# A hybrid pooling, state-space and mixture-of-experts layer: where the second half of the down matrices is fetched, and the last product and scaling by tiles

## The reference

```python
hx2 = modulate(rmsnorm(x, g_ffn), x_sh2, x_sc2)
eidx, gate = route(hx2, w_router, b_router)          # best group, two experts inside it
hid = silu(xb @ w_gate[e]) * (xb @ w_up[e])          # w_gate, w_up: 1024 x 512 per expert
y   = hid @ w_down[e]                                # w_down: 512 x 1024 per expert
x   = x + x_g2 * y                                   # y weighted by the two gates
return rmsnorm(x, g_final)                           # x * rsqrt(mean(x*x) + 1e-6) * g_final
```

## Time and profile before

| | us |
|---|---|
| median of 3 runs | 661.68 (659.23 to 661.77) |
| the profiled execution | 661.11 |
| its span, first to last instruction | 659.3 |
| TensorE busy | 588.4 (89%) |
| VectorE busy | 196.1 (30%) |
| ScalarE busy | 132.0 (20%) |
| GpSimd busy | 53.3 (8%) |

### The profile page before, as it was taken

The page is one execution under the profiler, slowest core; times in us unless marked ns, Lnnn a source line. Parts: engine busy times, 40 slices in busy tenths (PEclk is TensorE's granted clock), DMA queues, the critical chain, the costliest instruction groups (busy, mean ns, idle before and its releaser), DMA issues.

```text
span 659.3 us, 9355 instructions
## 1 busy us (share of the span) xinstructions
PE 588.4 (89%) x3770; PEld 249.9 (38%) x3770; DVE 196.1 (30%) x426; ACT 132.0 (20%) x226; POOL 53.3 (8%) x103
## 2 busy tenths in 40 slices
PE   1999968889899997899799879979997997899995
PEld 0454544455553342234233323423342342234331
DVE  7998458988730020002001000200100010002003
ACT  8661312031213111012020201111021102012111
POOL 3894000012010000000000000000000000000000
PEclk9999979999979999999799989989998999999999
DMA  8993999998779999999999999999999999999951
GB/s 330 418 402 110 319 327 292 401 410 351 299 281 409 422 419 421 422 417 422 422 421 420 423 421 421 420 421 422 422 422 422 423 421 421 421 421 375 403 227 64
DMA packets 43609, 249.02 MB, mean 378 GB/s; under 512 B 4776, under 2 KB 7480, under 8 KB 17216
## 3 DMA queue, kind: packets, MB, share of 16 engines
q1 hardware_dynamic: 41240, 243.93, 91.2%
q10 hardware_dynamic: 1992, 3.68, 1.7%
q0 software_dynamic: 352, 1.07, 0.5%
HBM read 244.46 MB, written 2.11 MB: 374 GB/s over the span
## 4 chain that ended last, share of the span: by engine, by line
PE 56%; DMA 21%; DVE 2%; issue 1%; SPq 0%; ACT 0%; POOL 0%; DVEq 0%
PE ps L863 21%; DMA wts<-in_w_up 21%; PE ps L903 17%; PE ps L835 5%; PE ps L841 5%; PE ps L799 2%; PE ps L711 1%; PE ps L879 1%; PE ps L759 1%; PE ps L727 1%; SPq L243 0%; PE ps L864 0%; DVE rc L1204 0%; DVE ra L1589 0%; PE ps L791 0%
## 5 line engine op out<-in xcount | busy, mean ns | idle before, releaser
L863 PE MATMUL ps<-wts,ra 128*64 128x512 f32 x512 | 242.5, 626 | 34.2 <-DMA wts<-in_w_up 33.0
L864 PE MATMUL ps<-wts,ra 128*64 128x512 f32 x512 | 242.6, 626 | 0.0
L863 PEld LDWEIGHTS ps<-wts,ra 128*64 128x64 f32 x512 | 70.0, 143 | 180.3 <-issue 133.5
L903 PE MATMUL ps<-wts,ra 128*32 128x512 f32 x512 | 111.4, 593 | 0.0
L903 PE MATMUL ps<-rc,ra 128*32 128x512 f32 x512 | 111.4, 593 | 0.0
L1204 DVE TENSOR_TENSOR ra<-ra,ps 128x256 f32<-128x256 f32 x32 | 13.5, 422 | 268.7 <-ACT ra L1150 268.6
L1144 ACT COPY ra<-ps 128x512 f32<-128x512 f32 x32 | 33.6, 1050 | 218.6 <-PE ps L864 218.6
L864 PEld LDWEIGHTS ps<-wts,ra 128*64 128x64 f32 x512 | 70.0, 143 | 0.0
L903 PEld LDWEIGHTS ps<-wts,ra 128*32 128x32 f32 x512 | 29.1, 110 | 73.2 <-issue 73.2
L1204 DVE TENSOR_TENSOR cb<-ps,ra 128x512 f32<-128x512 f32 x32 | 22.1, 692 | 103.4 <-PE ps L903 103.4
L1139 ACT COPY ra<-ps 128x512 f32<-128x512 f32 x32 | 18.8, 586 | 148.4 <-PE ps L835 148.4
(11 more groups left out here) (226 smaller groups left out, 509.4 us busy)
## 6 DMA issues: line engine op xcount, KB each, us to landing
wts<-in_w_up SPq DMA_DIRECT2D x64, 1024.0 KB, 15.5
wts<-in_w_gate SPq DMA_DIRECT2D x64, 1024.0 KB, 13.4
wts<-in_w_down SPq DMA_DIRECT2D x30, 1024.0 KB, 8.6
rc<-in_w_down SPq DMA_DIRECT2D x30, 1024.0 KB, 12.4
wts<-in_w_mod SPq DMA_DIRECT2D x16, 1024.0 KB, 13.4
r<-in_w_mod SPq DMA_DIRECT2D x6, 1024.0 KB, 10.9
wts<-in_w_out SPq DMA_DIRECT2D x2, 2048.0 KB, 11.5
wts<-in_w_in SPq DMA_DIRECT2D x2, 1024.0 KB, 19.8
```

The lines of the kernel that those rows point to most:

```text
L863: pe.matmul(ps[0:64, 4 + b, :], st, Wg[b][:, k, :], start=(k == 0), stop=(k == KD - 1))
L864: mm = pe.matmul(ps[64:128, 4 + b, :], st, Wu[b][:, k, :], start=(k == 0), stop=(k == KD - 1))
L903: mm = pe.matmul(ps[32 * j:32 * j + 32, BANKS[n], :], hid[:, j, f, SLOTS * t:SLOTS * t + SLOTS], Wd[j][:, f, 512 * h:512 * h + 512], start ...
```

## The change

1. SP's list. In the loop the second down halves of a round are issued behind experts three and four (j = 2, 3) of that round: `downs(i, 0)`, `second_two(i)`, `downs(i, 1)`, `next_two(i)`. In the last round both halves come behind them: `second_two(last_four)`, `downs(last_four, 0)`, then the pieces of f = 2 and f = 3.
2. In the last round the four tiles of each f are multiplied in the order 0, 2, 1, 3 (both halves of the first 128 tokens, then of the second), VectorE takes them in that order, and the last scatter is four matmuls, each of which waits for its own tile. The first square waits for two of them, the second for all four.
3. The final scaling is taken apart: VectorE multiplies by g_final and the constant 32 (the root of 1,024) as soon as the square of those tokens is read; the multiplication by the inverse root of the sum is done in a second step, three tiles on ScalarE and one on VectorE. GpSimd adds 1,024 times epsilon to the sum in place of dividing by 1,024. Three stores are SP's, one is ScalarE's.
4. Two semaphores of the start are one (`consts_set`), and `ss3_ready` is merged into `ss2_ready`.

```diff
@@ sync
             with sp.Fori(1, last_four) as i:
                 downs(i, 0)
+                second_two(i)
                 downs(i, 1)
-                second_two(i)
                 next_two(i)
+            second_two(last_four)
             downs(last_four, 0)
-            second_two(last_four)
             sp.wait_ge(S("down_mm"), 4 * last_four)
             for f in (2, 3):
                 down_load_one(sp, lambda j: (4 * last_four + j) % NE, f)
-            for t in range(NT):
-                sp.wait_ge(S("fin_ready"), 2 * t + 1)
-                store(sp, t, 0)
+            for h in range(2):
+                sp.wait_ge(S("fin_act"), h + 1)
+                store(sp, 0, h)
+            sp.wait_ge(S("fin_ready"), 1)
+            store(sp, 1, 1)
@@ gpsimd
-            gp.wait_ge(S("mhalf_set"), 1)
+            gp.wait_ge(S("consts_set"), 2)
...
+            gp.dma_start(gfb, g_final.rearrange("(a d) -> a d", a=1).broadcast_to([P, D])).then_inc(S("gf_in"), 16)
+            for t in range(NT):
+                gp.wait_ge(S("ss2_ready"), NT + t + 1)
+                gp.tensor_scalar(ms2[:, 2 + t:3 + t], ms2[:, 2 + t:3 + t], float(D * EPS), None, ALU.add).then_inc(S("ms2_ready"), 1)
+                gp.wait_ge(S("ms2_ready"), NT + t + 1)
+                gp.tensor_tensor(rstd2[:, 2 + t:3 + t], ms2[:, 2 + t:3 + t], mhalf, ALU.pow).then_inc(S("rstd2_ready"), 1)
@@ tensor
+            TILE_ORDER = (0, 2, 1, 3)
...
-                    for n in range(4):
+                    for n in (TILE_ORDER if last else range(4)):
...
-            pe.wait_ge(S("out_copy"), 4 * last_four + 6)
             pe.wait_ge(S("pt_copy"), last_four + 2)
-            scatter(0, True)
-            pe.wait_ge(S("out_copy"), 4 * last_four + 8)
-            for t in range(NT):
-                pe.matmul(ps[:, 2 * t + 1, :], PT[:, t, :], oS[:, 2 + t, :], start=False, stop=True,
+            for at, n in enumerate(TILE_ORDER):
+                h, t = n // 2, n % 2
+                pe.wait_ge(S("out_copy"), 4 * last_four + 5 + at)
+                pe.matmul(ps[:, 2 * t + h, :], PT[:, t, :], oS[:, n, :], start=False, stop=True,
                           skip_group_check=True).then_inc(S("y_ready"), 1)
@@ scalar
-            act.wait_ge(S("sil_zero"), 1)
+            act.wait_ge(S("consts_set"), 2)
...
-                act.wait_ge(S("y_ready"), t + 1)
+                act.wait_ge(S("y_ready"), 2 * t + 2)
...
-            for t in range(NT):
-                act.wait_ge(S("fin_ready"), 2 * t + 2)
-                store(act, t, 1)
+            for at, (t, h) in enumerate(((0, 0), (0, 1), (1, 0))):
+                act.wait_ge(S("rstd2_ready"), NT + t + 1)
+                act.wait_ge(S("gf_scaled"), at + 1)
+                v = xn2[:, t, 512 * h:512 * h + 512]
+                act.mul(v, v, rstd2[:, 2 + t:3 + t]).then_inc(S("fin_act"), 1)
+            act.wait_ge(S("fin_act"), 3)
+            store(act, 1, 0)
@@ vector
-            four_out(last_four)
+            four_out(last_four, (0, 2, 1, 3))
             dve.wait_ge(S("gf_in"), 16)
             for t in range(NT):
-                dve.wait_ge(S("rstd2_ready"), 3 + t)
+                dve.wait_ge(S("ss2_ready"), NT + t + 1)
                 for h in range(2):
                     c0 = slice(512 * h, 512 * h + 512)
-                    dve.scalar_tensor_tensor(xn2[:, t, c0], ps[:, 2 * t + h, :], rstd2[:, 2 + t:3 + t], gfb[:, c0],
-                                             ALU.mult, ALU.mult).then_inc(S("fin_ready"), 1)
+                    dve.scalar_tensor_tensor(xn2[:, t, c0], ps[:, 2 * t + h, :], ROOT_D, gfb[:, c0],
+                                             ALU.mult, ALU.mult).then_inc(S("gf_scaled"), 1)
+            dve.wait_ge(S("rstd2_ready"), 2 * NT)
+            dve.wait_ge(S("gf_scaled"), 2 * NT)
+            v = xn2[:, 1, 512:1024]
+            dve.tensor_scalar(v, v, rstd2[:, 3:4], None, ALU.mult).then_inc(S("fin_ready"), 1)
```

More of the change, by code:

```diff
@@ L1 @@
 import itertools
+import math
 from contextlib import ExitStack
@@ L69, in hybrid_block @@
     FC = F // P
+    ROOT_D = float(math.isqrt(D))
     NC = T // L
+    assert ROOT_D * ROOT_D == D
     DG = 32
@@ L486, in _ @@
             gp.dma_start(brb, b_router.rearrange("(a d) -> a d", a=1).broadcast_to([P, NE])).then_inc(S("br_in"), 16)
[L487 to L491, removed]
+            for t in range(NT):
+                gp.wait_ge(S("ss2_ready"), t + 1)
                 gp.tensor_scalar(ms2[:, t:t + 1], ms2[:, t:t + 1], 1.0 / D, EPS, ALU.mult, ALU.add).then_inc(S("ms2_ready"), 1)
@@ L836, in gather, with scatter @@
                 mm.then_inc(S("gather_mm"), 1)
-            def scatter(h, stop=False):
+            def scatter(h):
                 for t in range(NT):
-                    mm = pe.matmul(ps[:, 2 * t + h, :], PT[:, t, :], oS[:, 2 * h + t, :], start=False, stop=stop, skip_group_check=True)
-                return mm
+                    pe.matmul(ps[:, 2 * t + h, :], PT[:, t, :], oS[:, 2 * h + t, :], start=False, stop=False, skip_group_check=True)
             pe.wait_ge(S("g2_ready"), 1)
@@ L1181, in _ @@
             for t in range(NT):
-                act.wait_ge(S("y_ready"), t + 1)
+                act.wait_ge(S("y_ready"), 2 * t + 2)
                 if t:
-                    act.wait_ge(S("ss3_ready"), t)
+                    act.wait_ge(S("ss2_ready"), NT + t)
                 act.activation(ra[:, 4096:5120], ps[:, 2 * t:2 * t + 2, :].rearrange("p a n -> p (a n)"), ACT.Square,
-                               accum_out=ms2[:, 2 + t:3 + t]).then_inc(S("ss3_ready"), 1)
-            for t in range(NT):
-                act.wait_ge(S("fin_ready"), 2 * t + 2)
-                store(act, t, 1)
+                               accum_out=ms2[:, 2 + t:3 + t]).then_inc(S("ss2_ready"), 1)
+            for at, (t, h) in enumerate(((0, 0), (0, 1), (1, 0))):
[5 more added lines that the diff above has]
+            store(act, 1, 0)
             act.wait_ge(S("out_done"), 16 * 2 * NT)
@@ L1204, in tt @@
                 return dve.tensor_tensor(o, a, b, op)
-            dve.memset(sil[:, :], 0.0).then_inc(S("sil_zero"), 1)
-            dve.memset(mhalf, -0.5).then_inc(S("mhalf_set"), 1)
+            dve.memset(sil[:, :], 0.0).then_inc(S("consts_set"), 1)
+            dve.memset(mhalf, -0.5).then_inc(S("consts_set"), 1)
             dve.wait_ge(S("vec_in"), 16)
@@ L1564, in four_hidden, with four_out @@
                        ALU.mult).then_inc(S("hid_ready"), 1)
-            def four_out(i):
-                for n in range(4):
-                    dve.wait_ge(S("down_mm"), 4 * i + n + 1)
+            def four_out(i, order=range(4)):
+                for at, n in enumerate(order):
+                    dve.wait_ge(S("down_mm"), 4 * i + at + 1)
                     tt(oS[:, n, :], ps[:, BANKS[n], :], g2b[:, 512 * (n // 2):512 * (n // 2) + 512], ALU.mult).then_inc(S("out_copy"), 1)
```

## The result

The changed kernel takes 654.71 us (median of 6 runs, 652.86 to 657.86); the kernel before took 661.58 in the same comparison. The ratio is 0.991, with a 95% interval of 0.988 to 0.994, so 6.9 us faster (4.2 to 7.8 by the interval). I had forecast 654.1, with 651 to 657 around it. Its profiled execution took 654.72 us, with a span of 652.6.

A forecast was written before the change was run, and what follows sets the result against it. Transfers at 421 GB/s were taken to pace rounds 1 to 6, TensorE the last round. Fetching order 6.3 plus tiles and scaling 0.8 made 7.1 us off 661.11, 654.0, given as 654.1; range 651.0 to 657.0.

The forecast's parts named there:

- The order of fetching, 6.3 us: SP's list: moving down halves behind experts three and four ends the last down product at 642.8, before 649.07.
- A(0): First matmul after round 0's last wait for expert weights, at 216.53 in the profile before; the starting mark of the ledger.
- E: End of the last down product, where the last scatter starts; forecast 642.8, before 649.07.
- A(1): First matmul after round 1's last wait for expert weights; forecast 268.8 in place of 276.6, 7.8 us earlier.
- the dips: Transfer rate below 400 GB/s around 245 to 252 and 595 to 603, the queue partly dry, 2.1 us each.
- the transfers are over near 637.1: End of transfers in the kernel before; with one more dry spot of 2.1 us the last byte lands at 639.2.
- Tiles and scaling, 0.8 us: Kernel's end: last product by tiles and final scaling taken apart gain 0.8 us together, between 0.2 and 1.2.
- last store E + 6.9 in place of E + 7.7: Final scaling: the last output store is issued 6.9 us behind the last down product, before 7.7.
- (a): Rival: the queue does not dry up, expert weights come the full 9.96 us earlier; 650.4 us, chance 0.10.
- (b): Rival: last round's down weights later than the ledger, or clock falls in the wait; 655.3 to 657, chance 0.13.
- (c): Rival: queue shares bandwidth among all pieces, nothing is pulled forward, only 0.8 us come; 660.3 us, chance 0.05.
- (d): Rival: SP issues experts three and four late, rounds 2 to 6 each lose 2.1 us; 664.4 us, slower, chance 0.04.

The follow-up runs named there:

- the order alone: Kernel before with only SP's order of fetching changed, in the loop and the last round; 654.81 us, ratio 0.990.
- the second profile of the changed kernel: The changed kernel run once more, unaltered, on the same chip as a mark for comparison; 655.45 us.
- The half stores: Changed kernel with each of the four stores writing only 256 of its 512 columns; one execution, span ends at 651.0.
- the run with everything on VectorE: Changed kernel with all four final multiplications on VectorE, none on ScalarE; one execution, span ends at 652.6.
- the run with parts 2 and 3 alone: Changed kernel with SP's fetching order of the kernel before, keeping the product by tiles and the shared scaling; 660.73 us, ratio 1.000.
- one piece sent ahead: Changed kernel with one 1 MB piece of the last round's first down halves issued ahead of experts three and four; 652.74 us, ratio 0.988.
- the pieces lowered step by step: Changed kernel with five down pieces ahead of experts three and four in round 1, three in rounds 2 to 6, none in round 7; 649.93 us, ratio 0.982.
- the last round's move alone: Changed kernel with the loop fetching as before, only the last round's down halves behind experts three and four; 662.04 us, ratio 1.002.

## Why the prediction was right, point by point

**The order of fetching, 6.3 us.** Right in mechanism and nearly in size. Counted from A(0), E came 5.7 us earlier in the profile after, 5.9 with the order alone and 4.8 in the second profile of the changed kernel. Step by step: A(1) moved by 8.2 us (7.8 predicted), A(6)-A(0) by 7.6 (7.8), the round 6 to 7 took 52.2 as said, the wait for the first down halves was 1.65 us (1.5), and the dips stood where they were expected, lacking 2.2 us of transfer each (2.1). The wait did not bring the granted clock down, it is 1.00 behind it too, and so the 1.3 us kept for it were not needed:

```profile
628.00:632.00 4.00, 3.48 (x36) 1.33 (x39) 0.00 (x0) 0.00 (x0) 0.00 (x0) 1.00 1.03 416
```

What is short of 6.3 is mostly at the end, and one term of the sum is at fault there, "the transfers are over near 637.1". That is where the rate had fallen off. The kernel before has its last piece issued at 619.97, and it landed 18.0 us later:

```profile
rc<-in_w_down SPq DMA_DIRECT2D x1, 512.0 KB, 18.0
```

So the last byte was at 638.0, 0.9 us later than the term. With the predicted 2.1 added it is 640.1, where 639.2 was predicted; A(0) + 423.1 and 424.1 in the two profiles after are 639.7 and 640.6 on the prediction's clock. TensorE therefore waited for f = 3, 0.15 us in one profile and 0.74 in the other, where the sum has no wait. The rest is round 2, 60.0 us in place of 59.6, and a wait for the first halves of 1.65 in place of 1.5.

**Tiles and scaling, 0.8 us.** The step that failed is "last store E + 6.9 in place of E + 7.7". The instants were right: second square at E + 3.66 (3.7 to 3.8 predicted), g_final products from E + 3.2 and E + 4.8, the last multiplication ending at E + 6.7 (6.8). But the time of the last store's issue is not what ends the kernel. The four stores are 1.05 MB in a row, and from the first one's issue to the end of the span it is 4.5 us in the kernels before and after. The last one's issue moved by 1.0 us, from E + 7.7 to E + 6.7, but it landed 2.8 us later in place of 2.1, behind the others' bytes. The first store moved from E + 5.74 to E + 5.41, and so 0.3 us is the gain. The prediction put the transfer of the stores at nothing. The half stores show that bytes count in it, and the run with everything on VectorE that the first store moves the end (first store 1.3 us later, end 1.3 us later) where the last one's issue is as in the kernel before. The 0.3 us themselves are read from profiles; the times of the run with parts 2 and 3 alone show no difference. The other edits were free as said, but it is not the table load that waits for the first transfer: ScalarE's starts at 1.21 us before and 1.24 after, and the operation behind it at 2.65 in both.

**The sum.** 6.3 + 0.8 = 7.1 was forecast. In the spans it was 6.7: 5.7 by order, 0.3 at the end, and 0.7 because the expert part happened to begin that much earlier, which is not the change's doing. That the profile's total came within 0.7 us of the forecast 654.0 is in part luck, two terms too large (by 0.6 and 0.5) and a start that made up for most of it. The later comparison, 655.45 against 661.51, gives 6.1 us, which is closer to what the profiles put down to the change, 6.0.

**The rivals.** (a), a queue that does not dry up, falls with the dips at 242 and 594; made true in one place by one piece sent ahead, it gave 1.7 to 2.6 us. (b) holds in small: TensorE waits up to 0.7 us for the last piece. (c), that nothing is pulled forward, falls with A(1). Its doubt of the order holds in small: in the run with the pieces lowered step by step a 512 KB piece issued at 608.60 landed at 630.0, and the next one, issued at 610.84, at 629.3. (d), a dry spot in every round, did not occur: rounds 2 to 6 run at 59.6 with the same three waits. But its mechanism is real, and the last round's move alone shows it: eight us of empty queue and an end 2.9 us later than before.

## What to carry to other kernels

Where transfers and the computing engine are both nearly full, keep a ledger of the queue, piece by piece, beside the engine's own pace, and end it at the landing of the last piece and not where the rate falls off. A load that is moved behind another one helps only if the queue still has work when the engine releases the next buffer, and a gain in the loop can be given back whole by one load left in the old place in the last round: look at the first and the last round apart. At the end of a kernel, ask when the first byte of the output can leave, and not only when the last operation is done.

## What the runs showed of the hardware that was not expected

Issuing is not free when many transfers are queued. In the changed kernel SP's last down pieces took

```profile
L260 SPq DMA_DIRECT2D rc<-in_w_down x4: 1074/1992/2076, 611.2 to 621.1; - x4
```

(duration in ns, min, median, max), where an issue otherwise takes 0.33 to 0.38 us. The same happens in each of rounds 2 to 6 of the changed kernel, where the second down halves of the round are issued:

```profile
309.05 0.85 SPq L253 DMA_DIRECT2D wts<-in_w_down  x2
309.99 3.65 SPq L253 DMA_DIRECT2D rc<-in_w_down  x2
```

What these places share is the number of transfers outstanding, issued and not yet landed, and not their bytes or their time: ten of 1 MB at 309.99, where the new one landed 25 us later, and ten at 612.33, three of them of 512 KB, where it landed 21.6 us later. Counted over all eleven traces from 200 us on: of SP's 1,393 issues with at most eight outstanding 1,369 took less than 0.5 us and one took over 1 us; of 230 with ten or eleven outstanding 164 took over 1 us. In the kernel before only the last piece found ten outstanding, and it alone took over 1 us. What makes ten the number the runs do not say. It cost nothing visible here, since the rounds stayed at 59.6 us, but a list that has to issue something urgent behind so deep a queue would feel it.

A queue with 2.0 us of work left by the ledger lost about 2.2 us of transfer when the next loads came; one with 4.5 left lost nothing in one case, 0.9 in a second and 1.2 in a third. What sets this margin the runs do not say.
